# Experts: the gathers of u rows leave out the blank slots by a bounds check

## What is computed

```python
g_p, g_idx = lax.top_k(softmax(u @ w_rg + b_rg), 1)            # one group
e_p, e_idx = lax.top_k(softmax(logits of that group), 2)       # two experts in it
weight = g_p * e_p / sum(e_p)
# for each expert e with its rows xb of u:
y = (silu(xb @ w_gate[e]) * (xb @ w_up[e])) @ w_down[e]        # 1024x512, 1024x512, 512x1024
out[token] += y * weight                                       # both experts of a token
```

## Time and profile before

| what | value |
|---|---|
| median of three runs | 1615.62 us (1613.68 to 1619.09) |
| the profiled execution's own time | 1615.61 us |
| its span in the profile | 1613.5 us |
| PE busy | 1422.6 us (88%) |
| DVE busy | 951.5 us (59%) |
| ACT busy | 697.0 us (43%) |
| POOL busy | 613.8 us (38%) |
| expert stage (first gather to the last store of y) | 962 to 1562 us |
| DMA in the expert stage | 414 to 415 GB/s in most slices |

### The profile page before, as it was taken

One profiled execution on the slowest core, in us unless ns is written; L12 is line 12 of the kernel. 1 busy time (PEld: TensorE's weight loads), 2 busy tenths in 40 slices (PEclk: granted clock), 3 DMA queues, 4 the chain that ended last, 5 costly groups with the idle time before them and its releaser, 6 DMA issues. The chain is left out here.

```text
span 1613.5 us, 32405 instructions
## 1 busy us (share of the span) xinstructions
PE 1422.6 (88%) x14194; PEld 1224.2 (76%) x14194; DVE 951.5 (59%) x1004; ACT 697.0 (43%) x669; POOL 613.8 (38%) x198
## 2 busy tenths in 40 slices
PE   4999999999968999999998428999999999999930
PEld 4999999999967777776786226888888888888820
DVE  5446654543114565555655257778778777877717
ACT  4523442113212122221221015787787778777712
POOL 1001110000000000000000017999999999999934
PEclk9999999999968999999999658999999999999965
DMA  6134445433269334233311366999999999999756
GB/s 198 40 106 146 131 132 172 127 97 118 79 175 373 124 116 140 73 120 110 116 55 41 138 260 223 390 415 414 414 415 414 414 414 415 414 414 415 292 199 244
DMA packets 182034, 366.72 MB, mean 227 GB/s; under 512 B 10624, under 2 KB 70272, under 8 KB 180880
## 3 DMA queue, kind: packets, MB, share of 16 engines
q1 hardware_dynamic: 169248, 318.87, 54.2%
q0 software_dynamic: 6912, 25.17, 4.0%
q10 hardware_dynamic: 5760, 20.97, 3.2%
HBM read 296.01 MB, written 68.98 MB: 226 GB/s over the span
## 5 line engine op out<-in xcount | busy, mean ns | idle before, releaser
L1060 PE MATMUL ps<-u_hi,w_hi 128*128 128x352 f32 (+1 forms) x720 | 239.1, 332 | 6.9 <-DVE u_lo L711 6.9
L1060 PE MATMUL ps<-u_lo,w_hi 128*128 128x352 f32 (+1 forms) x720 | 234.9, 326 | 0.0
L1060 PE MATMUL ps<-u_hi,w_lo 128*128 128x352 f32 (+1 forms) x720 | 233.9, 325 | 0.0
L2378 POOL TENSOR_TENSOR down_lo<-down_raw,down_hi 128x1024 fp32r<-128x1024 f32 x32 | 178.5, 5579 | 31.5 <-ACT down_hi L2423 31.5
L2378 POOL TENSOR_TENSOR gate_lo<-gate_raw,gate_hi 128x1024 fp32r<-128x1024 f32 x32 | 177.1, 5535 | 10.1 <-ACT gate_hi L2423 10.1
L2506 DVE TENSOR_TENSOR down_lo<-down_raw,down_hi 128x3072 fp32r<-128x3072 f32 x32 | 109.4, 3420 | 97.1 <-ACT down_hi L2423 97.1
L2378 POOL TENSOR_TENSOR up_lo<-up_raw,up_hi 128x1024 fp32r<-128x1024 f32 x32 | 154.5, 4828 | 1.6 <-ACT up_hi L2423 1.0
L1060 PEld LDWEIGHTS ps<-u_hi,w_hi 128*128 128x128 f32 x720 | 138.6, 193 | 13.9 <-issue 10.6
L1374 POOL TENSOR_TENSOR mix_stat<-mix_stat,minus_half 128x4 f32<-128x4 f32 x8 | 8.1, 1006 | 351.4 <-DVE mix_stat L1589 351.4
L1060 PEld LDWEIGHTS ps<-u_hi,w_lo 128*128 128x128 f32 x720 | 138.4, 192 | 0.0
L1060 PEld LDWEIGHTS ps<-u_lo,w_hi 128*128 128x128 f32 x720 | 138.4, 192 | 0.0
(11 more groups left out here) (382 smaller groups left out, 2948.3 us busy)
## 6 DMA issues: line engine op xcount, KB each, us to landing
gate_raw<-in_moe_w_gate SPq DMA_DIRECT2D x32, 2048.0 KB, 13.1
up_raw<-in_moe_w_up SPq DMA_DIRECT2D x32, 2048.0 KB, 14.9
down_raw<-in_moe_w_down SPq DMA_DIRECT2D x32, 2048.0 KB, 13.5
tm_rows<-tm_stage SPq DMA_DIRECT2D x32, 512.0 KB, 3.3
y_slots<-y_out ACTq DMA_DIRECT2D x32, 512.0 KB, 6.8
w_raw<-in_w_in SPq DMA_DIRECT2D x30, 512.0 KB, 3.7
tm<-tm_rows SPq DMA_DIRECT2D x8, 1792.0 KB, 9.5
fm<-fm_rows SPq DMA_DIRECT2D x8, 1024.0 KB, 11.7
```

The costliest lines, as they stand in the source:

```text
L1060: mm = pe.matmul(z_of(n, r_), w[n % 3][:, k_, :], a[:, k_, c0:c1], start=(k_ == 0 and i == 0), stop=(k_ == KD - 1 and i == 2))
L2378: pool.tensor_tensor(lo[e % 2][:, cut:, :], raw[e % 2][:, cut:, :], hi[:, cut:, :].bitcast(F32), ALU.subtract).then_inc(sem(f"{name}_lo2_r ...
```

## The change

A constant `NO_ROW` = 4096 is taken from every entry of `row_no`, so that a filled slot sums to its row - 4096 and a blank one to 0. VectorE's cast into `slot_row` becomes an addition of 4096 with int32 output: filled slots have their row again, blank ones 4096. Both kinds of gather of u rows get a bounds check at row 1023 that isn't an error: rows beyond it are left out, and their places in `x_rows` keep what they held. GpSimd clears each of the two buffers once, ahead of gathers 0 and 1, and waits for each clear.

```diff
--- before.py
+++ after.py
@@ -30,6 +30,8 @@
 DE = 512
 KE = DE // P
 DECAY = math.exp(-0.5)
+
+NO_ROW = 4096
 EXTRA = (2 * SEQ - 1) // P
 NBLK = NE + EXTRA
 SUB = 16
@@ -121,7 +123,7 @@
     c["thresholds"] = (np.arange(8) + 1)[None, :] * P + np.zeros((P, 1))
     c["block_no"] = np.arange(EXTRA)[None, :] + np.zeros((P, 1))
     c["slot_no"] = np.arange(P)[None, :] + np.zeros((P, 1))
-    c["row_no"] = np.arange(NTX)[None, :] * P + p
+    c["row_no"] = np.arange(NTX)[None, :] * P + p - NO_ROW
     c["block_at"] = np.arange(NBLK + 1)[None, :] * P + np.zeros((P, 1))
     table, route = np.zeros((P, NCONST), np.float32), np.zeros((P, NROUTE), np.float32)
     for name, (a, b) in CONST_AT.items():
@@ -2231,7 +2233,7 @@
                     dve.tensor_copy(slots[:], slot_f[:]).then_inc(sem("slots_ready"), 1)
                     dve.wait_ge(sem("slots_ready"), 1)
                     dve.wait_ge(sem("slot_rows_done"), 1)
-                    dve.tensor_copy(slot_row[:], ps[:, 2, 0:NBLK]).then_inc(sem("slot_row_ready"), 1)
+                    dve.tensor_scalar(slot_row[:], ps[:, 2, 0:NBLK], float(NO_ROW), None, ALU.add, ALU.bypass).then_inc(sem("slot_row_ready"), 1)
                     dve.wait_ge(sem("slot_row_ready"), 1)
 
                 @block.scalar
@@ -2368,8 +2370,11 @@
 
                         if e >= 2:
                             pool.wait_ge(sem("x_turned"), e - 1)
-                        pool.indirect_dma_start(x_rows[e % 2][:], None, u2_dram, bass.IndirectOffsetOnAxis(ap=slot_row[:, e:e + 1], axis=0)
-                                                ).then_inc(sem(f"x_rows_loaded{e % 2}"), 16)
+                        else:
+                            pool.memset(x_rows[e][:], 0.0).then_inc(sem("x_rows_cleared"), 1)
+                            pool.wait_ge(sem("x_rows_cleared"), e + 1)
+                        pool.indirect_dma_start(x_rows[e % 2][:], None, u2_dram, bass.IndirectOffsetOnAxis(ap=slot_row[:, e:e + 1], axis=0),
+                                                bounds_check=SEQ - 1, oob_is_err=False).then_inc(sem(f"x_rows_loaded{e % 2}"), 16)
 
                     def low(name, e):
 
@@ -2394,8 +2399,8 @@
                     def more(n):
                         pool.wait_ge(sem("x_rows_loaded1"), 16 * NE // 2)
                         pool.wait_ge(sem("more_row_ready"), n)
-                        pool.indirect_dma_start(x_rows[0][:], None, u2_dram, bass.IndirectOffsetOnAxis(ap=more_row[:, 0:1], axis=0)
-                                                ).then_inc(sem("more_x_loaded"), 16)
+                        pool.indirect_dma_start(x_rows[0][:], None, u2_dram, bass.IndirectOffsetOnAxis(ap=more_row[:, 0:1], axis=0),
+                                                bounds_check=SEQ - 1, oob_is_err=False).then_inc(sem("more_x_loaded"), 16)
                     over_extra(pool, more)
```

## The result

The changed kernel takes 1622.03 us in the median of 11 runs (1613.13 to 1630.08), beside 1615.28 us for the kernel before in 11 runs (1610.38 to 1619.09). The ratio is 1.0043, with a 95% interval of 1.0027 to 1.0059: slower by 7 us, a little more than the 0.3% that was to be told from no change. The profiled execution took 1620.62 us, span 1618.6 us.

What follows compares the result with a forecast made beforehand. TensorE was taken to set the pace, 17.70 us an expert, with DMA queues full only because loads are issued early. Terms 0 + 0 + 0.6 + 0 = +0.6 us on 1615.61 us gave 1616.2 us, range 1613 to 1622.

Steps and rivals of the forecast that it cites:

- Fewer rows fetched: Expert stage's gathers: 8.4 MB less from queue 0, worth 0 us since no engine waits for a DMA there.
- The period named as a sign of being wrong: Steady expert stage: a period other than 17.71 us per expert would show the forecast wrong.
- The two readings that I set against it: Expert stage: no wait for a DMA listed; products 0.228 us apart without loads, 0.227 under full load; so TensorE sets the pace.
- The bounds check on GpSimd: Gathers on GpSimd in the expert stage: checked gathers take about 1 us, costing 0 us.
- The price I worked out: GpSimd's gather ahead of up_lo, steady part: any length up to 4.14 us costs 0; 5.59 us would cost 44 us.
- the first rival: Slower: steady-part gathers stopped by VectorE's subtraction last 4.39 us, 0.25 us over in 30 experts, +8 us, 1624 us; chance 0.10.
- The two clears: Stage start, ahead of gathers 0 and 1: +1.2 us for the first clear, -0.6 us for gather 0 landing sooner; +0.6 us.
- The second clear: Ahead of gather 1 at the start: hidden, since GpSimd may start gate_lo as late as 968.6 instead of 965.32.
- The addition in place of the cast: Ahead of the gathers, into slot_row: one operation of the same size replaces the 0.21 us cast, 0 us.
- The faster one: Expert stage: transfers set the pace, so 3.6% fewer bytes give -19 us, 1597 us; chance 0.04.
- A skipped row that costs the queue something: Gathers: blank rows still fetched or costing the queue as much; the 0.6 gain falls away, 1616.8 us; chance 0.05.
- The forecast of no change: Whole kernel: time the same within about 0.3% (4.8 us), chance 0.86; 0.81 for the course as forecast.

Runs made afterwards that it cites:

- the second profile: The changed kernel unaltered, timed and profiled again beside the follow-up kernels: ratio 1.0022 against the kernel before, stage 602.10 us.
- 7: The kernel before with half of every y_out stored a second time, 0.26 MB more per expert: ratio 1.0078, stage 612.14 us.
- 4: The changed kernel with filled and blank slots spread evenly over the partitions, the same 2048 rows left out: ratio 1.0000, stage 598.03 us.
- 5: The changed kernel with ranks 0 to 63 of a block placed in partitions 0 to 31 and 64 to 95: ratio 0.9994, stage 598.31 us.
- 6: The changed kernel with ranks 0 to 63 of a block placed in the even-numbered fours of partitions: ratio 1.0023, stage 601.74 us.
- 1: The changed kernel with NO_ROW = 0: clears and bounds check stay, blank slots fetch row 0, none left out: ratio 0.9998, stage 598.45 us.
- 3: The changed kernel with every slot naming a row past the table, so all gathered rows are left out: ratio 0.9994, stage 598.10 us.
- 10: The changed kernel with each gathered row 2 KB instead of 4 KB, blank slots still in the high partitions: ratio 1.0001, stage 598.09 us.

## Why the prediction was wrong

**Fewer rows fetched, 0 us: wrong.** This is the step that failed, with +7.8 us in the profiled execution (+3.9 in the second). I had "So the DMA queues are full because loads are issued early, and TensorE sets the pace". The second half holds, the first doesn't: a share of 1.04 and 414 GB/s were the limit (7). The period named as a sign of being wrong came, 18.34 us instead of 17.71 behind 1289.75 us, and the steady windows had 383 to 398 GB/s where 400 were to show the forecast right. The two readings that I set against it, no wait for a DMA and an equal distance of products, show only that the bound is TensorE. They don't show how much room is behind it, and a change that cuts into room without an owner in the list of waits needs just that. And I took 8.4 MB less to be at worst worthless, since the total fell. Not the total counts, but the fullest engine; by the map its bytes stayed, while packets got slower. That place decides is shown (4, 5 and 6 against the change); that a few per cent were missing is shown (7); why packets get slower is not.

**The bounds check on GpSimd, 0 us: right, for the wrong reason in part.** The length was about 1 us as taken. From the gathers of the changed kernel (min/median/max in ns; landing in us):

```profile
L2376 POOL DMA_INDIRECT x_rows<-u_rows,slot_row x32: 1005/1011/4067, 960.5 to 1487.2; - x32
...
DMA to landing us min/median/max: 4.4/7.7/11.1
```

The median is 1.011 us against 0.957. But the maximum of 4.067 us is what I had argued away by the gather at 1202.43, which "ran 0.87 us inside VectorE's subtraction". It had started 0.08 us ahead of it. In every expert of the steady part before, the gather started ahead of VectorE's subtraction, by as little as 0.03 us. Where a gather starts behind VectorE's two-input subtraction, it stops until that ends; the timeline of the changed kernel's start shows two such gathers:

```profile
957.37 0.21 DVE L2236 TENSOR_SCALAR slot_row<-ps 128x47 int32<-128x47 f32 x1 [7.01 <-PE ps L2258]
...
958.69 0.95 POOL L2374 MEMSET x_rows<- 128x1024 f32 x1 [56.41 <-POOLq L174]
...
960.54 1.20 POOL L2376 DMA_INDIRECT x_rows<-u_rows,slot_row  x1 [0.90 <-POOL x_rows L2374]
961.75 0.97 POOL L2374 MEMSET x_rows<- 128x1024 f32 x1
...
962.75 3.36 DVE L2511 TENSOR_TENSOR gate_lo<-gate_raw,gate_hi 128x3072 fp32r<-128x3072 f32 x1 [5.18 <-ACT gate_hi L2428]
963.50 3.47 POOL L2376 DMA_INDIRECT x_rows<-u_rows,slot_row  x1 [0.79 <-POOL x_rows L2374]
...
965.01 1.97 PE L2593 MATMUL ps<-consts,x_rows 128*128 128x128 f32 x8 [7.75 <-DMA x_rows<-u_rows,slot_row]
967.00 2.35 POOL L2383 TENSOR_TENSOR gate_lo<-gate_raw,gate_hi 128x1024 fp32r<-128x1024 f32 x1
...
969.22 3.37 DVE L2511 TENSOR_TENSOR up_lo<-up_raw,up_hi 128x3072 fp32r<-128x3072 f32 x1
...
969.51 0.76 PE L2600 MATMUL ps<-gate_hi,x_hi 128*128 128x512 f32 x1 [2.53 <-POOL gate_lo L2383]
969.52 3.95 POOL L2376 DMA_INDIRECT x_rows<-u_rows,slot_row  x1 [0.16 <-issue]
...
973.49 2.42 POOL L2383 TENSOR_TENSOR up_lo<-up_raw,up_hi 128x1024 fp32r<-128x1024 f32 x1
```

The gather at 963.50 starts inside VectorE's 962.75 to 966.11 and lasts until 966.97; that at 969.52 starts inside 969.22 to 972.59 and lasts until 973.47: each ends 0.9 us behind VectorE. The Trainium skill, page SBUF — State Buffer, section Who interferes with whom, says that whoever issues first gets the shared ports for the whole instruction. Where VectorE issues first the trace agrees, for gathers too, though the same section infers that a `tensor_tensor`, which this subtraction is, leaves the writing of descriptors alone. Where the gather issues first it doesn't agree: VectorE's subtraction at 1202.51 took its usual 3.36 us beside the gather. The price I worked out, nothing below 4.14 us, held at the start: in 1, 3, 4, 5 and 10 the gather that follows the first gate_lo lasted 3.95 or 3.96 us, and the stage was as long as before. It doesn't hold for gathers in the steady part that start behind VectorE: in 7 eight of 3.9 us came up to 1257.85 us, with 3.0 us lost, 0.4 us for each, where the first rival had 0.25 us.

**The two clears, +1.2 - 0.6 = +0.6 us: +0.01 us (+0.26 in the second profile).** The rows above: the clear takes 0.95 us (1.0 taken), GpSimd waits 0.90 us behind it (0.2 taken), yet the gather goes out only 1.1 us later against `slot_row`, 3.17 instead of 2.06 us, as the clear starts at 1.32 us, before the gather used to be issued. Against it the transposes start 4.5 us behind the gather instead of 5.6: 1.1 us and not 0.6. Within its bounds of -0.8 to +2.7. The second clear was called hidden. It is, but only just: with the gather behind it stopped by VectorE, gate_lo starts at 967.00, and the first product waits for it. In 4 the transposes came 1 us sooner (6.67 us) and the product didn't (12.04).

**The addition in place of the cast, 0 us: right.** 0.21 us both.

**The rivals.** The slower one was to be a long gather on GpSimd, +8 us. The sign and nearly the size came, by another mechanism: long gathers there are, ten behind 1288 us, but they start only once the loads are late. The faster one, "the transfers set the pace after all", was half true: they do as soon as they lose 3%, but giving bytes back yields nothing while TensorE is at 17.70 us an expert (4, 5). A skipped row that costs the queue something was named as a rival too, but only as a gain that falls away, with no price for the other transfers. The forecast of no change had 0.86 and the range ended at 1622.0, 0.03 us short of the median.

## What to carry to other kernels

When two resources look full, ask the second how much room it has (a few per cent more bytes tell in one run) before calling a change to it free. Bytes saved in a transfer count only where they relieve the fullest DMA engine: padding that lies together at the end of a tile left half of the engines as full as before here, so spread it, or leave it in (spreading avoided the loss, but gained no time). And whether two instructions exclude each other is to be read from a pair in which the one in question starts second.

## What the hardware showed beyond that

- A row left out by the bounds check still makes a packet of 4 bytes (6912 packets for 16.79 MB), and in each kernel with such rows packets, nearly all of other transfers, take longer than 159 or 84 ns, by 2.9 to 5.5% of the engines' time in all; without such rows none does.
- A gather that starts behind VectorE's two-input subtraction ends 0.9 us behind it, mostly after 3.95 us instead of 1.01, with a bounds check or without (3.9 instead of 0.96 us in 7). One that starts ahead of it, be it by 0.03 us, takes its usual time, and so does VectorE.
- Once the loads are late, SP's instruction that issues a load of gate is itself held, up to 2.754 us instead of 0.37; in the kernel before, at 414 GB/s, it never was (0.393 us at most).
